# A large transformer-style kernel on one core: gate and up projection by seven half-block products in place of eight

## The reference, cut to what matters

```
h = rmsnorm(x, ffn_norm[l])
gu = h @ w_gate_up[l]                  # 512 x 1024 times 1024 x 5632
gt, up = jnp.split(gu, 2, axis=-1)     # 2816 columns each
x = x + (jax.nn.silu(gt) * up) @ w_down[l]
return rmsnorm(x, final_norm)
```

## Time and profile before

| | us |
|---|---|
| time, median of 3 runs | 3879.58 (3879.27 to 3880.35) |
| profiled execution, its own time | 3876.03 |
| its span, first to last instruction | 3874.2 |
| TensorE busy | 3743.9 (97% of the span) |
| VectorE busy | 1544.0 (40%) |
| ScalarE busy | 1268.4 (33%) |
| GpSimd busy | 873.4 (23%) |
| matmuls of `gu` (line 1478) | 302.4 |
| matmuls of `down` (line 1489) | 151.3 |

### The profile page before, as it was taken

One profiled execution on the slowest core, in us unless ns is written; L12 is line 12 of the kernel. 1 busy time (PEld: TensorE's weight loads), 2 busy tenths in 40 slices (PEclk: granted clock), 3 DMA queues, 4 the chain that ended last, 5 costly groups with the idle time before them and its releaser, 6 DMA issues.

```text
span 3874.2 us, 50481 instructions
## 1 busy us (share of the span) xinstructions
PE 3743.9 (97%) x21034; PEld 2112.6 (55%) x21034; DVE 1544.0 (40%) x2770; ACT 1268.4 (33%) x2333; POOL 873.4 (23%) x888
## 2 busy tenths in 40 slices
PE   7999999999999999999999999999999999999998
PEld 3565655655655545677667754444555544444443
DVE  2434332223332111777777761354777721110001
ACT  3444443222232022444444440675444511000000
POOL 0000000101100000666666660122445420000000
PEclk9999999999999999999999999999999999999999
DMA  5111002010002111111111011121101011212121
GB/s 213 48 63 71 31 23 87 22 66 35 31 33 87 65 60 66 45 45 45 45 45 43 15 60 63 57 92 71 45 29 45 32 63 58 105 65 87 59 75 52
DMA packets 24242, 226.40 MB, mean 58 GB/s; under 512 B 2640, under 2 KB 5200, under 8 KB 8784
## 3 DMA queue, kind: packets, MB, share of 16 engines
q1 hardware_dynamic: 24016, 223.18, 15.6%
HBM read 221.07 MB, written 2.10 MB: 58 GB/s over the span
## 4 chain that ended last, share of the span: by engine, by line
PE 91%; DVE 4%; ACT 1%; DMA 1%; issue 1%; POOL 1%; DVEq 0%; SPq 0%; POOLq 0%; ACTq 0%
PE bank L1172 9%; PE bank L1478 8%; PE bank L1119 6%; PE bank L1182 5%; PE bank L933 4%; PE bank L1030 4%; PE bank L886 4%; PE bank L1489 4%; PE bank L1295 3%; PE bank L1162 3%; PE bank L872 3%; PE bank L1055 2%; PE bank L952 2%; PE bank L1086 2%; PE bank L1254 2%; PE bank L1434 2%
## 5 line engine op out<-in xcount | busy, mean ns | idle before, releaser
L1172 PE MATMUL bank<-hT,ring 128*128 128x256 f32 (+1 forms) x1024 | 349.8, 490 | 0.0
L1478 PE MATMUL bank<-hT,ring 128*128 128x512 f32 x704 | 302.4, 592 | 2.4 <-DVE hT L2057 2.4
L1172 PEld LDWEIGHTS bank<-hT,ring 128*128 128x128 f32 x1024 | 189.6, 190 | 122.0 <-issue 108.1
L1119 PE MATMUL bank<-Y,ring 128*128 128x512 f32 (+1 forms) x704 | 247.8, 515 | 0.0
L1478 PEld LDWEIGHTS bank<-hT,ring 128*128 128x128 f32 x704 | 133.7, 190 | 171.1 <-issue 170.1
L1119 PEld LDWEIGHTS bank<-Y,ring 128*128 128x128 f32 x704 | 133.8, 190 | 113.8 <-issue 107.1
L933 PE MATMUL bank<-hT,ring 128*128 128x256 f32 (+1 forms) x512 | 186.3, 501 | 2.4 <-ACT hT L1564 2.4
L1295 PE MATMUL bank<-hT,ring 128*128 128x512 f32 x384 | 178.9, 600 | 4.7 <-ACT Y L1570 4.7
L886 PE MATMUL bank<-hT,ring 128*128 128x256 f32 (+1 forms) x512 | 182.3, 493 | 0.0
L1182 PE MATMUL bank<-ring,hT 128*128 128x128 f32 x1536 | 182.0, 277 | 0.0
L1182 PEld LDWEIGHTS bank<-ring,hT 128*128 128x128 f32 x1536 | 176.3, 192 | 2.1
(11 more groups left out here) (412 smaller groups left out, 6821.7 us busy)
## 6 DMA issues: line engine op xcount, KB each, us to landing
ring<-in_w SPq DMA_DIRECT2D x60, 2048.0 KB, 8.2
ring<-in_w SPq DMA_DIRECT2D x17, 1536.0 KB, 7.2
ring<-in_w SPq DMA_DIRECT2D x20, 1280.0 KB, 5.5
ring<-in_w SPq DMA_DIRECT2D x12, 1024.0 KB, 4.9
ring<-in_w SPq DMA_DIRECT2D x8, 1408.0 KB, 6.0
ring<-in_w SPq DMA_DIRECT2D x19, 512.0 KB, 3.5
xT<-in_xT SPq DMA_DIRECT2D x1, 3072.0 KB, 11.7
out<-arena SPq DMA_DIRECT2D x8, 256.0 KB, 2.2
```

The costliest lines, as they stand in the source:

```text
L1119: ins = e.matmul(m[:, 0:b - a], w[:, k, sl(j % 2)], src[:, k, a:b], start=k == 0, stop=k == kt - 1)
L1172: ins = e.matmul(m[:, 0:b - a], w[:, k, sl(1 + d)], hT[:, k, a:b], start=k == 0, stop=k == 7)
L1478: ins = e.matmul(m, w[:, k, sl(2 * i + j % 2)], hT[:, k, 0:LAT], start=k == 0, stop=k == 7)
```

## The change

In the tiles 1 to 21 the product is cut into half blocks: the eight blocks of the inner dimension into a lower and an upper four, the tokens into two halves of 256. With gate weights G1, G2, up weights U1, U2 (lower and upper) and h as h11 (lower, first tokens), h12 (lower, second tokens), h21, h22 (upper), the eight products of half blocks become seven (a Strassen-Winograd scheme):

- once, by VectorE (`gu_t`): T0 = h12 - h11, T1 = h22 - T0, T2 = h22 - h12, T3 = h21 - T1, each 1024 elements per partition;
- for each tile, by VectorE (`gu_s`): S0 = U1 + U2, S1 = S0 - G1, S2 = G1 - U1, S3 = G2 - S1, each 512 elements per partition, in one of two buffers;
- for each tile, by TensorE (`gu`): seven products in the order a = G1 h11, b = S1 T1, d = S2 T2, c = S0 T0, a += G2 h21, d += U2 T3, c += S3 h22, each 4 matmuls of 128x128 weights by 256 tokens, into the lower half of four banks (0 to 3 for even j, 4 to 7 for odd j);
- ScalarE copies a out after the first product (`gu_p1`), and does two SiLU of 256 tokens in place of one of 512;
- VectorE (`gu`) joins the results with five additions of 256 elements, two of which (`gu_u` 1 and 2) read d and c before TensorE adds the next product to the same bank; the multiplication by up (`gu_p`) is done one tile later, in the midst of the next tile's additions.

`gate_up_steps` sets the order: the sums of the weights of tile j+1 stand on VectorE ahead of the additions of tile j. `down(0)` waits for each product only where it reads it.

```diff
             + [("nh", n, s, k) for s in range(NORM_PARTS[n]) for k in range(8)])
 
 
+def gate_up_steps():
+    made = [("gu", 0), ("gu_t",), ("gu_s", 1)]
+    for j in range(1, 22):
+        made += [("gu_s", j + 1)] * (j < 21) + [("gu", j)]
+    return made + [("gu_p", 21)]
 NORM_PARTS = [2, 2, 1, 1, 1]
...
-         + [("tables",)] + norm_tiles(3, "wo") + norm_rest(3) + [("gu", j) for j in range(22)]
+         + [("tables",)] + norm_tiles(3, "wo") + norm_rest(3) + gate_up_steps()
...
+    "gu_vec": ("gu_prod", "gu_s", "gu_t", "gu_u"),
+    "gu_act": ("gu_p1", "gu_silu"),
...
+        gu_S = [arena_[:, 2048 * i:2048 * i + 2048].rearrange("p (n k c) -> p n k c", n=4, k=4) for i in range(2)]
+        gu_T = arena_[:, 4096:8192].rearrange("p (n k t) -> p n k t", n=4, k=4)
+        gu_1, gu_2, gu_g = ([arena_[:, 11264 + o + 256 * i:11520 + o + 256 * i] for i in range(2)] for o in (0, 512, 1024))
+        gu_up = [arena_[:, 12800 + 512 * i:13312 + 512 * i] for i in range(2)]
+        HALF = [slice(0, 256), slice(256, 512)]
+        def gu_factors(j):
+            a = spot["gu_slab", j // 2] % NRING * SLOT
+            w = ring[:, a:a + 4096].rearrange("p (k n) -> p k n", k=8)
+            return w[:, :, sl(j % 2)], w[:, :, sl(2 + j % 2)]
 
         def tensor(e):
...
             def gu(j):
-                w = open_w["gu"][0] if j % 2 else slab("gu", 8)
-                for i in range(2):
-                    m = take(proj, ("gu", j, i), ("gu_silu" if i == 0 else "gu_prod", j))
-                    for k in range(8):
-                        if j == i == 0:
-                            q.wait_ge(*on(*h_tile(3, 0, k)))
-                        ins = e.matmul(m, w[:, k, sl(2 * i + j % 2)], hT[:, k, 0:LAT], start=k == 0, stop=k == 7)
-                    ins.then_inc(up("gu_mm", (j, i)), 1)
+                if j % 2 == 0:
+                    slab("gu", 8)
+                    spot["gu_slab", j // 2] = open_w["gu"][1]
+                g, u = gu_factors(j)
+                if j == 0:
+                    for i, w in enumerate((g, u)):
+                        m = take(proj, ("gu", j, i), ("gu_silu", (j, 1)) if i == 0 else ("gu_prod", j))
+                        for k in range(8):
+                            if i == 0:
+                                q.wait_ge(*on(*h_tile(3, 0, k)))
+                            ins = e.matmul(m, w[:, k], hT[:, k, 0:LAT], start=k == 0, stop=k == 7)
+                        ins.then_inc(up("gu_mm", (j, i)), 1)
+                    return
+                sums, (h1, h2) = gu_S[j % 2], HALF
+                a, b, c, d = (take(4 * (j % 2) + n, ("gu", j, n), token)[:, 0:256] for n, token in enumerate(
+                    (("gu_silu", (j, 0)), ("gu_u", (j, 0)), ("gu_u", (j, 4)), ("gu_u", (j, 3)))))
+                for n, (m, l, r, first, token) in enumerate((
+                        (a, g[:, 0:4], hT[:, 0:4, h1], True, None),
+                        (b, sums[:, 1], gu_T[:, 1], True, ("gu_s", (j, 1))),
+                        (d, sums[:, 2], gu_T[:, 2], True, ("gu_s", (j, 2))),
+                        (c, sums[:, 0], gu_T[:, 0], True, None),
+                        (a, g[:, 4:8], hT[:, 4:8, h1], False, ("gu_p1", j)),
+                        (d, u[:, 4:8], gu_T[:, 3], False, ("gu_u", (j, 1))),
+                        (c, sums[:, 3], hT[:, 4:8, h2], False, ("gu_u", (j, 2))))):
+                    if n == 1:
+                        q.wait_ge(*on("gu_t", 3))
+                    if n == 6:
+                        q.wait_ge(*on("gu_s", (j, 3)))
+                    if token:
+                        q.wait_ge(*on(*token))
+                    for k in range(4):
+                        ins = e.matmul(m, l[:, k], r[:, k], start=first and k == 0, stop=k == 3, skip_group_check=True)
+                    ins.then_inc(up("gu_mm", (j, n)), 1)
                 if j % 2:
-                    give("gu", "gu_mm", (j, 1))
+                    give("gu", "gu_mm", (j, 6))
 
             def down(j):
                 w = slab("down", 22)
-                if j == 0:
-                    q.wait_ge(*on("gu_prod", 21))
                 m = take(proj, ("down", j), ("down_x", j))
                 for k in range(22):
+                    if j == 0:
+                        q.wait_ge(*on("gu_prod", k))
                     ins = e.matmul(m, w[:, k, :], yf[:, k, :], start=k == 0, stop=k == 21)
                 ins.then_inc(up("down_mm", j), 1)
                 give("down", "down_mm", j)
...
 
             def gu(j):
                 q.wait_ge(*on("gu_mm", (j, 0)))
-                e.activation(yf[:, j, :], bank[spot["gu", j, 0]], ACT.Silu).then_inc(up("gu_silu", j), 1)
+                if j == 0:
+                    e.activation(yf[:, j, :], bank[spot["gu", j, 0]], ACT.Silu).then_inc(up("gu_silu", (j, 1)), 1)
+                    return
+                if j >= 3:
+                    q.wait_ge(*on("gu_u", (j - 2, 0)))
+                e.activation(gu_1[j % 2], bank[spot["gu", j, 0]][:, 0:256], ACT.Copy).then_inc(up("gu_p1", j), 1)
+                q.wait_ge(*on("gu_mm", (j, 4)))
+                e.activation(yf[:, j, 0:256], bank[spot["gu", j, 0]][:, 0:256], ACT.Silu).then_inc(up("gu_silu", (j, 0)), 1)
+                q.wait_ge(*on("gu_u", (j, 4)))
+                e.activation(yf[:, j, 256:512], gu_g[j % 2], ACT.Silu).then_inc(up("gu_silu", (j, 1)), 1)
 
             do = {"start": start, "tables": tables, "ns": ns, "nq": nq, "nr": nr, "nh": nh, "zabs": zabs,
                   "zc": lambda j: z("zc", j, yc, BOTH[:1]), "zcs": lambda: z("zc", 15, yc, BOTH[:1]), "dz": lambda j, c: c == 3 and z("dz", j, yd, BOTH[:1]), "na_sq": na_sq_,
...
                 q.wait_ge(*on("wo_mm", j))
                 e.tensor_tensor(xT[:, j, 0:LAT], bank[spot["wo", j]], xT[:, j, 0:LAT], ALU.add).then_inc(up("wo_x", j), 1)
 
+            def gu_t():
+                (h1, h2), lo, hi = HALF, slice(0, 4), slice(4, 8)
+                q.wait_ge(*on("h_scaled", (3, 0, 7)))
+                e.tensor_tensor(gu_T[:, 0], hT[:, lo, h2], hT[:, lo, h1], ALU.subtract).then_inc(up("gu_t", 0), 1)
+                q.wait_ge(*on("gu_t", 0))
+                e.tensor_tensor(gu_T[:, 1], hT[:, hi, h2], gu_T[:, 0], ALU.subtract).then_inc(up("gu_t", 1), 1)
+                e.tensor_tensor(gu_T[:, 2], hT[:, hi, h2], hT[:, lo, h2], ALU.subtract).then_inc(up("gu_t", 2), 1)
+                q.wait_ge(*on("gu_t", 1))
+                e.tensor_tensor(gu_T[:, 3], hT[:, hi, h1], gu_T[:, 1], ALU.subtract).then_inc(up("gu_t", 3), 1)
+            def gu_s(j):
+                g, u = gu_factors(j)
+                i, s = spot["gu_slab", j // 2], gu_S[j % 2]
+                q.wait_ge(*on(f"w{i % NRING}", i))
+                if j == 1:
+                    q.wait_ge(*on("wo_mm", 7))
+                if j >= 3:
+                    q.wait_ge(*on("gu_mm", (j - 2, 6)))
+                e.tensor_tensor(s[:, 0], u[:, 0:4], u[:, 4:8], ALU.add).then_inc(up("gu_s", (j, 0)), 1)
+                q.wait_ge(*on("gu_s", (j, 0)))
+                e.tensor_tensor(s[:, 1], s[:, 0], g[:, 0:4], ALU.subtract).then_inc(up("gu_s", (j, 1)), 1)
+                e.tensor_tensor(s[:, 2], g[:, 0:4], u[:, 0:4], ALU.subtract).then_inc(up("gu_s", (j, 2)), 1)
+                q.wait_ge(*on("gu_s", (j, 1)))
+                e.tensor_tensor(s[:, 3], g[:, 4:8], s[:, 1], ALU.subtract).then_inc(up("gu_s", (j, 3)), 1)
+            def gu_p(j):
+                q.wait_ge(*on("gu_silu", (j, 1)))
+                if j == 0:
+                    q.wait_ge(*on("gu_mm", (j, 1)))
+                else:
+                    q.wait_ge(*on("gu_u", (j, 3)))
+                e.tensor_tensor(yf[:, j, :], yf[:, j, :], gu_up[j % 2] if j else bank[spot["gu", 0, 1]],
+                                ALU.mult).then_inc(up("gu_prod", j), 1)
             def gu(j):
-                q.wait_ge(*on("gu_silu", j))
+                if j == 0:
+                    return
+                b, c, d = (bank[spot["gu", j, n]][:, 0:256] for n in (1, 2, 3))
+                s, (u1, u2) = gu_2[j % 2], (gu_up[j % 2][:, h] for h in HALF)
+                q.wait_ge(*on("gu_p1", j))
                 q.wait_ge(*on("gu_mm", (j, 1)))
-                e.tensor_tensor(yf[:, j, :], yf[:, j, :], bank[spot["gu", j, 1]], ALU.mult).then_inc(up("gu_prod", j), 1)
+                if j >= 3:
+                    q.wait_ge(*on("gu_u", (j - 2, 4)))
+                    q.wait_ge(*on("gu_prod", j - 2))
+                e.tensor_tensor(s, b, gu_1[j % 2], ALU.add).then_inc(up("gu_u", (j, 0)), 1)
+                q.wait_ge(*on("gu_u", (j, 0)))
+                q.wait_ge(*on("gu_mm", (j, 2)))
+                e.tensor_tensor(u2, d, s, ALU.add).then_inc(up("gu_u", (j, 1)), 1)
+                q.wait_ge(*on("gu_u", (j, 1)))
+                q.wait_ge(*on("gu_mm", (j, 3)))
+                e.tensor_tensor(u2, c, u2, ALU.add).then_inc(up("gu_u", (j, 2)), 1)
+                gu_p(j - 1)
+                q.wait_ge(*on("gu_mm", (j, 5)))
```

(7 more changed lines are left out.)

## The result

The changed kernel takes 3845.5 us (median of 4 runs, 3840.0 to 3849.7) where the kernel before takes 3879.4 (median of 4). The ratio is 0.9912, with a 95% interval from 0.9894 to 0.9929: 34 us faster, in an interval of 28 to 41. Taken over all runs of both, 13 and 21, the means are 3846.4 and 3880.2, a difference of 33.8 us. Forecast were 3844.3 us and a gain of 35.3.

A forecast was written before the change was run, and what follows sets the result against it. TensorE's matmul stream was taken to bound gate and up. Cheaper products (34.3 us) and an earlier start of `down` (1.0) gave 35.3 us off 3879.6, so 3844.3 us; range 3841 to 3853.

The forecast's parts named there:

- The price of a half-sized record: TensorE, tiles 1 to 21 of gate and up: 0.2157 us per 256-token record, 1176 records in 253.7 us.
- The price of the whole record: TensorE, gate and up before the change: 286.26 / 668 = 0.4285 us per 512-token record, 288.0 us for 672.
- The seam: Where `down` follows gate and up: `down` no longer waits for the last product at its start, gain 1.0 us.
- The cover: In gate and up, VectorE's and ScalarE's new work hides behind TensorE's products; about 2.66 us to spare, added waits cost nothing.
- Both rivals that lived on VectorE: VectorE bounds gate and up (3889 us, 0.02), or additions come late by part of a microsecond (0.09, shared with bared loads).
- The rival of fulfilled waits that break the lead of the loads: Gate and up: each wait exposes a 0.19 us weight load, 16 us in all, time 3860; chance 0.09, shared with late additions.
- The rival of loads that bind: Gate and up: each half-sized record costs load plus stream, 0.406 us, time 4068; chance 0.01.
- forecast of no stall: Gate and up: TensorE never waits for VectorE or ScalarE, at 0.2157 us a record; chance 0.85.

The follow-up runs named there:

- two split forms: Kernel before, each gate and up matmul split into two of 256 tokens, halves alternating or one after the other: 0.2156 and 0.2158 us a record.
- second split form: Kernel before, each gate and up matmul split into two of 256 tokens, one half of the tokens after the other: 0.2158 us a record.
- twelve idle sums: Changed kernel with twelve unused additions of 512 elements ahead of each tile's weight sums on VectorE: 3927.1 us.

## Why the prediction was right

**The price of a half-sized record, the step that carries the sum: right.** Forecast 0.2157 us; the 1176 records of tiles 1 to 21 took 253.8 us, 0.2158 each. Taking the distance between starts and not the page's busy time per record was what mattered: with the 0.234 or 0.241 of the earlier trace rows the gain would have come out as 13 or 5 us. The two split forms of the old kernel confirm the price apart from all the rest of the change. That a matmul of the code is two records, on which the 32 and 56 a tile rest, the counts show: 704 records for 22 x 16 matmuls before, 1176 for 21 x 28 after.

**The price of the whole record: 0.0006 us too small.** I divided the 286.26 us between two loads by 668, but 668 is the number of loads with both ends counted, and there are 667 distances: 0.4292 us. The old tiles 1 to 21 are 288.4 us and not 288.0, so the term is 34.6 and not 34.3.

**The seam: right**, 1.1 us forecast as 1.0, and shown alone in the old kernel. (That the last product is "hidden sixteen times over" was a slip: 18 us against 2 is nine times, or 16 us to spare.)

**The cover: right, but its edge was misread.** I had 2.66 us to spare at the second and third addition; it is 2.76. VectorE's total was overestimated (125 us forecast for the stage; 104 in the 21 tiles and some 14 in tile 0), since operations that do not wait for one another start 0.60 us apart though each is drawn as 0.685. Both rivals that lived on VectorE were tried: 2.4 us more of it a tile cost nothing, taking 2.6 away gained nothing, and 7.3 more cost the 2.8 us a tile that the timeline gives. The rival of fulfilled waits that break the lead of the loads is out: the 1176 records of tiles 1 to 21 start 0.2158 us apart through all such waits, as the 1205 of the second split form of the old kernel do. Waits that truly hold do cost about 0.1 us beyond their length (24 records in 5.45 us for 5.34, eight in 1.99 for 1.89).

What was wrong is the sentence that TensorE begins to stall when the four sums and two additions grow by 2.66 us. That is how much later the second addition may end; the sums in front of it may grow by more, since VectorE first uses up its own waits for products b and d. By the rows of the changed kernel that is 2.76 + 0.57 + 1.30 = 4.6 us, and the twelve idle sums bear it out: they take 7.35 us and delay the sixth product by 2.71, so 4.6 were hidden. The forecast of no stall did not hang on it.

**The rival of loads that bind is refuted.** It priced a record at its load plus its stream, 0.406 us; measured is 0.2158. The 1176 loads, of 0.190 us and 128x128 each, lie in a stream that has no gap (PEld 223.5 us busy within 253.9 us of matmuls). The range also took in 3845 us, the time at a dearer half-sized record. No run shows that price: the runs showed 0.2158 us for the half and 0.4292 for the whole, a gain of 34.6 us in the 21 tiles.

**What I had not counted is the clock.** For the stage I read 1.00 before and forecast 1.00 after; in tile 0 it was 0.5 for some 5.7 us, 2.9 us lost, which 3.0 us of luck earlier in the launch made good in the profiled run. That the spans lie 36.0 us apart, so near to the forecast, is in this part luck; the 34.6 and the 1.1 are not. It is no effect of the change: the old kernel with split matmuls (0.5 from about 3404 to 3411 us) and the one with only the seam changed (0.63 and 0.52 in two windows of 2 us) have it as well, in a stage that begins with the same gap. The single profile of before, on which I built, was the one without. So the times, whose means over all runs are 33.8 us apart, agree with a gain of 35.7 us in the stage within the few microseconds by which the clock moves both kernels from run to run.

## What to carry to other kernels

Where a stage is one unbroken stream of large matmuls and VectorE is idle beside it, an eighth of the stream can be had by a seven-product scheme, if the half-sized record costs half (here 0.2158 us of 0.4292) and every sum has its place: one tile ahead for the sums of weights, behind a whole product for the additions that TensorE waits for. Price a matmul by the distance between starts in an unbroken run, count distances and not records, and lay the other engines' work along one tile on TensorE's time: the least spare time, here 2.76 us, says how much later a result may come, and with the waits that VectorE itself has before it, 4.6 us here, how much more work it can bear. Gaps in TensorE's stream should be avoided twice over, since a clock of 0.50 may come with them, as in eleven of the twelve profiles that have the gap before tile 0.

## What the runs showed of the hardware

- In the idle gap of 2.4 us before tile 0 (with one of 0.6 us shortly before it), the granted clock fell to 0.50 in eleven of the twelve profiles of kernels that have this gap: for 6.8 us in ten of them, most of it within tile 0, and for 3.4 in one. With the longer gap filled by idle matmuls it stayed at 1.00, in the one profile taken. Why one profile with the gap kept 1.00 is open.
- With an idle gap of 2.56 us in every tile the mean clock of the stage was 0.92, which cost 25 us beyond the gaps themselves; with matmuls that start 0.27 us late in every tile of 12.5 us it stayed at 1.00.
- The spread of both kernels' runs, about 12 us over all of them, goes in large part with the clock: two profiles of the same changed kernel, 11.0 us apart, have the same 253.8 us in this stage, and the runs' mean clocks lie between 0.987 and 0.991, by and large the higher the shorter the run. It does not account for all of it: the changed kernel with the old seam ran at 0.990 and took 3848.2 us, where the shortest run at 0.990 took 3840.0 and the seam is worth only 1.9 of the difference.
- VectorE operations of 512 elements that do not wait for one another start 0.60 us apart, though each is drawn as 0.685 (in the tile above at 3456.46, 3457.07 and 3457.67 us).
